# Attention over pairs of heads, on row tiles and column tiles of the TensorE array

## What is computed

```python
def chunked_attention(q, k, v, rel_table):
    ...
    s = jnp.einsum('bnqhd,bnkhd->bhnqk', qc, kb).astype(jnp.float32) * (HEAD_DIM ** -0.5)
    s = s + bias[None, :, None]
    s = jnp.where(valid[None, None, :, None, :], s, -1e30)
    p = jax.nn.softmax(s, axis=-1).astype(v.dtype)
    o = jnp.einsum('bhnqk,bnkhd->bnqhd', p, vb)
    return o.reshape(B, S, H * Dh)

def reference(...):
    for l in range(DEPTH):
        ...
        qh = rms_norm(q.reshape(B, S, N_HEADS, HEAD_DIM), q_gain[l])
        kh = rms_norm(k.reshape(B, S, N_HEADS, HEAD_DIM), k_gain[l])
        y_b = chunked_attention(qh, kh, vh, rel_table[l]) @ w_up_b[l]
        x = x + (gate_a * y_a + gate_b * y_b) @ w_out[l]
        ...
```

## Time and profile before

| what | value |
|---|---|
| median of 3 runs | 2779.78 us (2779.47 to 2781.95) |
| the profiled execution | 2780.0 us, its span 2778.2 us |
| PE busy | 2734.7 us (98%) |
| ACT, POOL, DVE busy | 43%, 42%, 30% |
| granted TensorE clock | 0.996 |
| attention, first transposes to last half of up_b | 857.36 to 951.27 us in layer 0, the same length in layer 1 |

### The profile page before, as it was taken

How to read it: one execution, slowest core, us unless ns; L and a number is a source line. 1 busy time by engine, 2 the same in 40 slices (tenths; PEclk the granted TensorE clock), 3 DMA queues, 4 the chain that set the end, 5 groups by cost and what they waited for, 6 DMA issues and landing times.

```text
span 2778.2 us, 35532 instructions
## 1 busy us (share of the span) xinstructions
PE 2734.7 (98%) x11968; PEld 2196.4 (79%) x11968; DVE 833.2 (30%) x1515; ACT 1188.3 (43%) x1680; POOL 1179.1 (42%) x524
## 2 busy tenths in 40 slices
PE   7999999999999999999999999999999999999998
PEld 6888878878776688888888888788787757888887
DVE  4222035630015432221132211448100164322212
ACT  5443235742445534443243432457324364444422
POOL 3444444445442234444444444344453423444444
PEclk9999999999999999999999999999999999999999
DMA  7333223332331233332333323332333212333322
GB/s 259 99 91 102 94 85 97 91 100 84 98 98 41 71 91 99 98 98 91 100 99 98 92 91 99 87 93 84 110 96 97 72 40 88 95 91 99 98 92 91
DMA packets 247056, 263.82 MB, mean 95 GB/s; under 512 B 9040, under 2 KB 233072, under 8 KB 246928
## 3 DMA queue, kind: packets, MB, share of 16 engines
q1 hardware_dynamic: 242768, 253.70, 30.6%
q10 hardware_dynamic: 4160, 8.47, 0.9%
HBM read 259.95 MB, written 10.57 MB: 97 GB/s over the span
## 4 chain that ended last, share of the span: by engine, by line
issue 40%; PE 40%; POOL 18%; DVE 1%; POOLq 1%; ACT 0%; DMA 0%; DVEq 0%; ACTq 0%
POOL wlo L414 18%; PE ps L1095 10%; PE ps L1100 10%; PE ps L1099 10%; PE ps L1295 2%; PE ps L1223 2%; PE ps L1277 1%; PE ps L1208 1%; PE ps L1244 1%; PE ps L1239 1%; PE ps L1243 1%; POOLq L421 0%; POOLq L413 0%; PE ps L1325 0%; DVE p L1013 0%
## 5 line engine op out<-in xcount | busy, mean ns | idle before, releaser
L414 POOL TENSOR_TENSOR wlo<-raw,whi 128x1024 fp32r<-128x1024 f32 x475 | 1140.7, 2408 | 1464.1 <-ACT whi L463 1463.7
L1095 PE MATMUL ps<-h_lo,whi 128*128 128x512 f32 x2400 | 945.9, 394 | 21.8 <-DVE h_lo L748 9.8
L1100 PE MATMUL ps<-h_hi,wlo 128*128 128x512 f32 x2400 | 936.5, 390 | 0.0
L1099 PE MATMUL ps<-h_hi,whi 128*128 128x512 f32 x2400 | 936.4, 390 | 0.0
L463 ACT ACTIVATE whi<-raw 128x1024 fp32r<-128x1024 f32 x475 | 500.2, 1056 | 737.3 <-PE ps L1095 676.4
L1095 PEld LDWEIGHTS ps<-h_lo,whi 128*128 128x128 f32 x2400 | 452.0, 188 | 126.9 <-DVE h_lo L748 14.9
L1099 PEld LDWEIGHTS ps<-h_hi,whi 128*128 128x128 f32 x2400 | 452.4, 188 | 96.6 <-issue 3.8
L1100 PEld LDWEIGHTS ps<-h_hi,wlo 128*128 128x128 f32 x2400 | 452.0, 188 | 94.9
L1095 PE MATMUL ps<-act_lo,whi 128*128 128x512 f32 x704 | 273.9, 389 | 0.0
L1099 PE MATMUL ps<-act_hi,whi 128*128 128x512 f32 x704 | 273.9, 389 | 0.0
L1100 PE MATMUL ps<-act_hi,wlo 128*128 128x512 f32 x704 | 273.9, 389 | 0.0
(11 more groups left out here) (139 smaller groups left out, 2635.6 us busy)
## 6 DMA issues: line engine op xcount, KB each, us to landing
raw<-in_w_in SPq DMA_DIRECT2D x124, 512.0 KB, 3.7
raw<-in_w_gate SPq DMA_DIRECT2D x88, 512.0 KB, 3.7
raw<-in_w_up SPq DMA_DIRECT2D x88, 512.0 KB, 3.7
raw<-in_w_down SPq DMA_DIRECT2D x80, 512.0 KB, 3.4
raw<-in_w_up_b SPq DMA_DIRECT2D x19, 512.0 KB, 3.6
rel_band<-rel_rows ACTq DMA_DIRECT2D x1, 8192.0 KB, 39.7
raw<-in_w_out SPq DMA_DIRECT2D x16, 512.0 KB, 3.4
raw<-in_rg_band SPq DMA_DIRECT2D x14, 512.0 KB, 3.5
```

What stands on the lines that cost most here:

```text
L414: nc.gpsimd.tensor_tensor(wlo[:, s, :], raw[:, s, :], whi[:, s, :].bitcast(F32), ALU.subtract).then_inc(lo_made, 1)
L1095: ins = pe.matmul(ps[:, b, :], w_hi, x_lo, start=start, stop=False)
L1099: pe.matmul(ps[:, b, :], w_hi, x_hi, start=False, stop=False)
L1100: return pe.matmul(ps[:, b, :], w_lo, x_hi, start=False, stop=stop)
```

## The change

Attention goes over pairs of heads t = 0 to 7, with e = 0, 1 for the two heads of a pair. Head e has its q and k in partitions 64e to 64e + 63 of the pair's tile.
- **Scores** use q and k as they lie, 64 rows each: head 0 on the upper row tile of the array, head 1 on the lower, one after the other in program order. POOL's copies of q to `square` are gone. `score_bank` gives each head two banks, so block rows 3 and 2 (`LATE`) come first, and 1 and 0 (`EARLY`) only when DVE has read all four banks.
- **Transposes** (`turn`) of head 0 go to bank 4, of head 1 to bank 5, in three rounds (4, 4 and 2 blocks), each of which waits until its bank of the round before is copied. ACT copies head 0's, DVE head 1's. Before, three banks took all of one head, and ACT copied all.
- **The product with v** (`weighted`) writes head 0 to partitions 0 to 63 of bank 6, head 1 to 64 to 127, and alternates between them.
- **Normalisation** is divided: the `LATE` block rows are multiplied on POOL, the `EARLY` ones on DVE.
- The pair's `prob` tiles are both in use for one pair; nothing holds a second pair. The transposes of pair t wait for both parts of the normalisation of t; the scores of t + 1 come after the transposes of t.
- The bias has three buffers in place of two. SP refills after a whole pair's exponentials.
- The output goes to tiles `o_hi`, `o_lo`, which lie where q and k were, in place of `h_hi`, `h_lo`. `gb_out` is still a tile and a stage of its own; tiles are laid out anew. The first half of up_b comes after the last pair, not between heads.

```diff
...
-TURNED = [(4, 0, KS * P, (0,)), (5, KS * P, KS * P, (1, 3)), (7, 2 * KS * P, 2 * P, (2,))]
+TURNED = [(0, KS * P, (0,)), (KS * P, KS * P, (1, 3)), (2 * KS * P, 2 * P, (2,))]
+LATE, EARLY = (3, 2), (1, 0)
+BANDS_HELD = 3
...
+        pt = [[pt0[:, at:at + width] for at, width, _ in TURNED],
+              [square[:, 0, :], square[:, 1, :], pt1_tail[:, :]]]
+        bias_of = [tmp[:, 0, :], tmp[:, 1, :], band2[:, :]]
...
+        def score_bank(e, i):
+            return 2 * e + i % 2
+        TURN_BANK, OUT_BANK = (4, 5), 6
...
-                    if head >= 2:
-                        sp.wait_ge(exp_made, C.next(exp_made, KS))
...
+                for t in range(KD - 1):
+                    sp.wait_ge(exp_made, C.next(exp_made, 2 * KS))
+                    for head in range(BANDS_HELD + 2 * t, min(BANDS_HELD + 2 * (t + 1), HEADS)):
+                        band_of(head)
...
-                        pool.wait_ge(prob_made, C.next(prob_made, KS))
-                    if head:
-                        pool.wait_ge(q_placed, C.now(q_placed))
-                    p_ = head % 2 * HD
-                    zeros = ones_head[p_:p_ + HD, HD - p_:HD - p_ + 1].to_broadcast([HD, S])
-                    nc.gpsimd.tensor_tensor(square[p_:p_ + HD, head % 2, :], q[p_:p_ + HD, head // 2, :], zeros,
-                                            ALU.add).then_inc(q_placed, C.made(q_placed))
...
+                def late(t):
+                    pool.wait_ge(inv_made, C.next(inv_made))
+                    nc.gpsimd.tensor_tensor(carrier_late[:, t:t + 1], ident[0:1, 0:1], ident[0:1, 0:1], ALU.add)
+                    for i in LATE:
+                        for e in range(2):
+                            part = prob[e][:, tri(i):tri(i + 1)]
+                            nc.gpsimd.tensor_scalar(part, part, inv[:, e, i:i + 1], None, ALU.mult
+                                                    ).then_inc(late_prob, C.made(late_prob))
+                    C.step(inv_made)
...
+                ring(-1)
+                ring(0)
+                late(0)
+                ring(1)
+                ring(2)
+                for t in range(1, KD):
+                    late(t)
...
+                def exps(blocks):
+                    for i in blocks:
+                        for e in range(2):
+                            b = score_bank(e, i)
+                            C.step(bank_read[b])
+                            act.wait_ge(bank_read[b], C.now(bank_read[b]))
+                            part = prob[e][:, tri(i):tri(i + 1)]
+                            nc.scalar.activation(part, part, ACT.Exp, scale=-1.0, bias=mx[:, e, i:i + 1],
+                                                 accum_out=total[:, e, i:i + 1]).then_inc(exp_made, C.made(exp_made))
...
+                for t in range(KD):
+                    for part in pt[0]:
+                        act.wait_ge(turned[0], C.next(turned[0]))
+                        nc.scalar.activation(part, ps[:, TURN_BANK[0], 0:part.shape[1]], ACT.Copy
+                                             ).then_inc(bank_read[TURN_BANK[0]], C.made(bank_read[TURN_BANK[0]]))
+                    if t + 1 < KD:
+                        exps(LATE)
+                        exps(EARLY)
+                    act.wait_ge(heads_out, C.next(heads_out))
+                    nc.scalar.activation(o_hi[:, t, :], ps[:, OUT_BANK, :], ACT.Copy
+                                         ).then_inc(split_hi, C.made(split_hi))
...
+                    for i in blocks:
+                        for e in range(2):
+                            b = score_bank(e, i)
+                            dve.wait_ge(scored, C.next(scored))
+                            nc.vector.memset(carrier[0:1, (2 * t + e) * KS + i:(2 * t + e) * KS + i + 1], 0.0)
+                            nc.vector.tensor_tensor_reduce(prob[e][:, tri(i):tri(i + 1)], ps[:, b, 0:(i + 1) * P],
+                                                           bias_of[(2 * t + e) % BANDS_HELD][:, S - (i + 1) * P:S], -1.0,
+                                                           3e38, ALU.add, ALU.min, mx[:, e, i:i + 1]
+                                                           ).then_inc(bank_read[b], C.made(bank_read[b]))
+                def inverted(blocks):
+                    at = slice(min(blocks), max(blocks) + 1)
+                    dve.wait_ge(exp_made, C.next(exp_made, 2 * len(blocks)))
+                    nc.vector.reciprocal(inv[:, :, at], total[:, :, at]).then_inc(inv_made, C.made(inv_made))
+                def early():
                     dve.wait_ge(inv_made, C.now(inv_made))
-                    for i in range(KS):
-                        part = prob[e][:, tri(i):tri(i + 1)]
-                        nc.vector.tensor_scalar(part, part, inv[:, e, i:i + 1], None, ALU.mult
-                                                ).then_inc(prob_made, C.made(prob_made))
+                    for i in EARLY:
+                        for e in range(2):
+                            part = prob[e][:, tri(i):tri(i + 1)]
+                            nc.vector.tensor_scalar(part, part, inv[:, e, i:i + 1], None, ALU.mult
+                                                    ).then_inc(early_prob, C.made(early_prob))
...
-                for head in range(HEADS):
-                    if head + 1 < HEADS:
-                        normalised(head + 1)
-                    if head + 2 < HEADS:
-                        biased(head + 2)
...
+                for t in range(KD):
+                    C.step(bank_read[TURN_BANK[0]], 3)
+                    for part in pt[1]:
+                        dve.wait_ge(turned[1], C.next(turned[1]))
+                        nc.vector.tensor_copy(part, ps[:, TURN_BANK[1], 0:part.shape[1]]
+                                              ).then_inc(bank_read[TURN_BANK[1]], C.made(bank_read[TURN_BANK[1]]))
+                    if t + 1 < KD:
+                        biased(t + 1, LATE)
+                        biased(t + 1, EARLY)
+                        inverted(LATE)
+                    if t + 1 < KD:
+                        inverted(EARLY)
+                        early()
+                    dve.wait_ge(split_hi, C.next(split_hi))
...
-                        pe.matmul(ps[:, i, 0:(i + 1) * P], square[:, head % 2, i * P:(i + 1) * P],
-                                  k[:, t, 0:(i + 1) * P], start=True, stop=True).then_inc(for_dve, C.made(for_dve))
...
+                    for i in blocks:
+                        for e in range(2):
+                            b = score_bank(e, i)
+                            pe.wait_ge(bank_read[b], C.now(bank_read[b]))
+                    for i in blocks:
+                        for e in range(2):
+                            head = slice(e * HD, (e + 1) * HD)
+                            pe.matmul(ps[:, score_bank(e, i), 0:(i + 1) * P], q[head, t, i * P:(i + 1) * P],
+                                      k[head, t, 0:(i + 1) * P], start=True, stop=True
+                                      ).then_inc(scored, C.made(scored))
+                            C.step(bank_read[score_bank(e, i)])
...
+                        if (half, a) == (1, 0):
+                            pe.wait_ge(qk_made, C.next(qk_made, 2 * KD))
+                            scores(0, LATE)
...
+                            scores(0, EARLY)
...
+                def turn(g):
+                    _, _, keys = TURNED[g]
+                    for e in range(2):
+                        pe.wait_ge(bank_read[TURN_BANK[e]], C.now(bank_read[TURN_BANK[e]]))
+                        at = 0
+                        for j in keys:
+                            for i in range(j, KS):
+                                ins = pe.transpose(ps[:, TURN_BANK[e], at:at + P],
+                                                   prob[e][:, tri(i) + j * P:tri(i) + (j + 1) * P], ident[:, :])
+                                at += P
+                        ins.then_inc(turned[e], C.made(turned[e]))
+                        C.step(bank_read[TURN_BANK[e]])
...
+                        for j in keys:
+                            for e in range(2):
+                                head = 2 * t + e
+                                ins = pe.matmul(ps[e * HD:(e + 1) * HD, OUT_BANK, j * P:S],
+                                                v[:, j, head * HD:(head + 1) * HD], pt[e][g][:, at:at + (KS - j) * P],
+                                                start=j == 0, stop=j == TURNED[-1][2][-1])
...
+                for t in range(KD):
+                    pe.wait_ge(late_prob, C.next(late_prob, 2 * len(LATE)))
+                    pe.wait_ge(early_prob, C.next(early_prob, 2 * len(EARLY)))
+                    turn(0)
+                    turn(1)
+                    turn(2)
+                    if t + 1 < KD:
+                        scores(t + 1, LATE)
+                    if t + 1 < KD:
+                        scores(t + 1, EARLY)
+                    weighted(t)
...
```

(44 more changed lines are left out.)

183 lines of the change are left out of this document (66 added, 117 removed).

## The result

| | before | changed kernel |
|---|---|---|
| median | 2780.8 us | 2853.5 us (2850.6 to 2855.4) |
| ratio | | 1.026 [1.0245, 1.0274] |
| profiled execution, span | 2780.0, 2778.2 us | 2850.6, 2848.8 us |
| granted clock, mean | 0.996 | 0.978 |

What follows compares the result with a forecast made beforehand. Attention was taken as TensorE-bound before, then bound by a closed chain of 12.9 us a pair; 7 x 12.9 + 12.4 - 93.9 - 1.9 = 6.9 us a layer, 13.8 in two, gives 2794 us, range 2774 to 2818.

Steps and rivals of the forecast that it cites:

- a closed chain whose last link is POOL: Attention pair: one set of tiles puts softmax between scores and transposes; POOL's multiplication ends the period, 12.3 to 14 us; 50%.
- period at full clock: Attention, from one pair's first transposes to the next pair's: 12.9 us, where PE took 11.4 before.
- last pair to up_b's second part: End of attention: turning, product with v to 6.8, then 24 products of up_b, 5.5; in all 12.4 us.
- LATE's multiplication: Normalising LATE rows on POOL, priced like the selection: four multiplications take 3.0 us, from 9.45 to 12.45.
- rival 1: POOL's multiplication quick, at filling's price, DVE hardly held: period 11.6 to 12.2, 2776 to 2784 us, no change; 20%.
- The stall between DVE and POOL: EARLY's multiplications on DVE fall into POOL's and slip between its instructions: some 0.45 us with the hand-off.
- rival 4: TensorE's clock falls to 1.2 GHz with pauses near 2 us: 2860 us throughout, 2820 upward in part; 10%.
- Rival 2: Faster: POOL quick, PE's hand-offs in turning and the exponentials' start shorter; period 11.3, 2771 us; 10%.
- Rival 3: Two heads' tiles on TensorE don't overlap in scores or product with v: period 13.7, 2813 us; 10%.
- Scores in the v projection: Scores placed among v products: delay falls from 4.3 to 2.4 us for the pair, 1.9 us saved.
- Change of tile shape: Between transposes and scores on PE: contained in the scores' start at 3.7 us, no further cost.

Runs made afterwards that it cites:

- experiment 2: Changed kernel with 24 unread products a pair added on PE, 6 between the two parts of the scores, 18 in its wait for POOL: 2826.9 us.
- experiment 1: Changed kernel with LATE's four multiplications moved from POOL to DVE, behind the reciprocals: 2790.7 us, ratio 1.0035.
- experiment 5: Changed kernel with a second set of probability tiles, fourth band buffer, two-stage queue order and POOL's two-input multiplication: 2742.8 us, ratio 0.986.
- experiment 3: Changed kernel with POOL's LATE multiplication written as a two-input operation, the inverse repeated along the row: 2818.0 us in one execution.
- experiment 6: Changed kernel with two sets of probability tiles, fourth band buffer and new queue order, but POOL's multiplication by a scalar operand kept: 2752.8 us, ratio 0.989.
- Experiment 4: Kernel before, one head at a time, with only the scores changed to 64 rows straight from q and k, without POOL's copies: 2788.5 us, ratio 1.0026.

## Why the prediction failed in size

The direction was right and so was the mechanism: a closed chain whose last link is POOL. By its own steps, in us after the first transposes of a pair:

| Step | forecast | measured |
|---|---|---|
| scores start after the turning rounds | 3.7 | 3.66 (859.64) |
| DVE reads the first scores | 4.82 | 4.82 (860.80) |
| ACT starts exponentials | 5.6 | 5.55 (861.53) |
| EARLY's scores start | 7.2 | 7.25 (863.23) |
| LATE's reciprocals done | 9.2 | 9.27 |
| POOL starts to multiply | 9.45 | 9.52 (865.50) |
| EARLY's exponentials done | 10.1 | 10.29 |
| POOL's four multiplications | 3.0 (1.9 to 3.7) | **5.57** |
| DVE's EARLY multiplications done | 11.5, later beside POOL | 12.72 |
| period at full clock | 12.9 | **15.14** |
| last pair to up_b's second part | 12.4 | 12.1 at full clock (experiment 2), 13.5 in the changed kernel |

- **The term that was mis-sized** is "LATE's multiplication": 3.0 us for what took 5.57. I took the slope of the selection in the earlier trace rows because it has one input and an operation, and held the two-input copy for the dearest. Measured, the slope is 2.5 ns a column (1569 less 1246 ns over 128), above both. The bound did not hold: none of the three rows had a multiplication with a scalar for each row, and POOL's price does not follow the number of inputs. The chance of a dearer operation had to widen the range. The rule of line rate for one input in the Trainium skill, GPSIMD Engine Reference §4.1, weighed there as rival 1, is further off: at the price of filling, which the prediction set beside that rule, four would take 1.9 us.
- **The stall between DVE and POOL** was added at 0.45 with the hand-off. In the changed kernel it costs the chain nothing: DVE's four take 2.19 us beside POOL and 1.01 without it (experiments 1 and 5), so they end at 12.72, but POOL ends later still, at 15.09, and PE starts 0.05 after POOL. With POOL's start 0.07 late and its part 2.57 too long, that leaves 15.14 - 12.9 = 2.24 us. The stall itself is real: in experiments 3 and 6, where POOL ends sooner, DVE's stretched multiplications are the last link.
- **The clock** (rival 4, 10%) came with the pause. The forecast looked at pauses near 2 us, and there it nearly held: in experiment 1, with pauses of 1.6 and 1.8, most pairs ran at full clock. The mistake was to keep it as a case of its own, priced at nothing in the sum. It hangs on the same term: the dearer POOL, the longer the pause, the lower the clock. A period of 15.14 in place of 12.9 costs 2 x 7 x 2.24 = 31 us directly and 26.6 more through the clock. The result, 2853.5, lies within rival 4's 2820 to 2860, but that is luck: rival 4 got there by the clock alone, and the clock's part is 26.6 of the 72.7.
- **Rival 1** (POOL out of the way, 2776 to 2784) is near experiment 1, though DVE does POOL's work there: a pair took 12.09, inside that rival's 11.6 to 12.2, and the time was 2790.7, with two pairs that the lower clock made longer. **Rival 2** (P = 11.3) has nothing for it: with LATE's multiplication out of the chain altogether the estimate is 11.65, which is the 11.6 that the prediction gave as the floor. **Rival 3** (no overlap) is ruled out by products that start 0.01 us apart, and by LATE's scores in 1.77 us.
- **Scores in the v projection** saved less than was said. PE's timeline of the changed kernel, against the earlier trace rows: the scores, and the second product behind them, as there.

```profile
835.30 1.77 PE L1267 MATMUL ps<-k,q 64*128 64x512 f32 x8
...
837.34 0.40 PE L1288 MATMUL ps<-whi,h_hi 128*128 128x512 f32 x1
...
842.66 0.92 PE L1267 MATMUL ps<-k,q 64*128 64x256 f32 x8
...
843.85 0.40 PE L1288 MATMUL ps<-whi,h_hi 128*128 128x512 f32 x1
```

  Less one product of 0.23 each, as in the prediction, that is 1.81 + 0.96 = 2.8 us a pair, where 2.4 was forecast, and the product ahead of each part takes 0.09 longer. So 1.4 us are saved in place of 1.9, as the first transposes show: they start at 855.98 in place of 857.36. In two layers that adds 1 us; the last pair, 12.1 in place of 12.4, takes 0.6 back.
- **Change of tile shape** was put at nothing beyond the 3.7. Experiment 4 puts it near 0.1 us each; the step into the scores lies in the measured 3.66.

Of the 72.7 us, 14 are the loss as forecast, 31 come from POOL's term, less the stall that cost nothing, and 27 from the clock.

## What to carry over

Where two units of work share all buffers of a stage, their chain is closed, and a faster engine only waits longer: ask first whether the buffers still hold the next unit, since with two sets and an order made for them the same tiles gave 1.4%. Bound an operation that no row shows by more than its neighbours when it ends the chain, and join to each such term what a longer pause does to TensorE's clock. An operation's price counts by its place: POOL's slow form cost 35 us at the end of a closed chain and 10 in a pipelined one, there mostly through DVE, which it held up. And where an engine waits for two others, compare their ends with its start before believing the releaser that a view names.

## What the runs showed of the hardware

- POOL's multiplication with one scalar for each row takes 1569 ns for 128 x 512 and 1246 for 128 x 384; as an operation with two inputs, the scalar repeated along the row, 1031 and 862 (818 in experiment 5).
- DVE's four EARLY multiplications (128 x 256 and 128 x 128, two of each) take 1.01 us alone. With POOL at work beside them they take 2.19 beside its form with a scalar and 2.93 beside its form with two inputs.
- Two heads on two halves of the array, fp32: LATE's scores 1.77 us, EARLY's 0.92, the product with v 2.3 us a pair, with starts 0.01 us apart.
- Entering and leaving the 64-row products costs about 0.1 us each.
- With pauses of 1.81 and 4.67 us in each pair of 16 to 18 us, the granted clock was 0.69 to 0.84, so in part the lower level, 1.2 GHz; the same pauses filled with unread products gave 1.00 and 26.6 us back.
